# A two-block transformer layer pair on one core: the head of the first block's mixers and of the second block's heads in another order

## The reference, cut to what matters

```python
# block 1: projection of the normed rows; iw are 8 columns per token, g_lr 16
h = rmsnorm(x, norm1_g)
qa, ka, va, iq, ik, iw, qb, kb, vb, g_lr, r_gate = split(h @ w_in)
idx_logits = einsum('bqhd,bsd->bqhs', iq, ik) * IDX_DIM ** -0.5
score = einsum('bqhs,bqh->bqs', relu(idx_logits), iw * IDX_HEADS ** -0.5)
_, idx = top_k(where(causal, score, -inf), 128)           # the keys that attention may see
log_a = log_sigmoid(g_lr @ gla_gate_w2 + gla_gate_b) / 16 # gates of the linear attention
...
# block 2
h = rms_norm(x, g_mix_norm) * (1 + scale_m) + shift_m
q_lat, kv_lat, k_rope, fq, fk, fv, f_logit, gate_a, gate_b = split(h @ w_in_2)
q = rms_norm(q_lat, g_q_lat) @ w_q_up ;  kv = rms_norm(kv_lat, g_kv_lat) @ w_kv_up
q_pe, k_pe = apply_rope(q[..., 64:], positions), apply_rope(k_rope, positions)
cum_log_f = cumsum(log_sigmoid(f_logit + b_forget), axis=1)
```

## Time and profile before

| | before |
|---|---|
| median of 3 runs | 2066.33 us (2064.2 to 2068.21) |
| the profiled execution | 2064.85 us |
| its span in the profile | 2063.0 us, so 1.85 us lie around it |
| PE, DVE, ACT, POOL busy | 92%, 59%, 46%, 30% |
| mean granted clock of TensorE | 0.957 of full |

### The profile page before, as it was taken

How to read it: one execution, slowest core, us unless ns; L and a number is a source line. 1 busy time by engine, 2 the same in 40 slices (tenths; PEclk the granted TensorE clock), 3 DMA queues, 4 the chain that set the end, 5 groups by cost and what they waited for, 6 DMA issues and landing times. The chain is left out here.

```text
span 2063.0 us, 27185 instructions
## 1 busy us (share of the span) xinstructions
PE 1893.1 (92%) x8330; PEld 1306.0 (63%) x8330; DVE 1208.6 (59%) x2231; ACT 953.0 (46%) x1630; POOL 609.2 (30%) x467
## 2 busy tenths in 40 slices
PE   6999998989999995899999969899999999999992
PEld 3534447867777663677678857477766676666661
DVE  1666317367777764563353334477777777776773
ACT  2411227336666553463453222266655565555551
POOL 4797715012222222770100000012222222222221
PEclk9699999989999997999989989999999999999996
DMA  5353410639999964412112354379999999999983
GB/s 183 123 173 104 162 44 12 264 125 332 332 332 333 328 223 149 163 42 91 38 42 86 119 190 177 112 262 343 338 335 324 328 342 332 331 321 330 321 275 103
DMA packets 121435, 441.70 MB, mean 214 GB/s; under 512 B 32036, under 2 KB 36532, under 8 KB 83976
## 3 DMA queue, kind: packets, MB, share of 16 engines
q1 hardware_dynamic: 93672, 406.94, 53.4%
q0 software_dynamic: 27648, 33.67, 7.3%
q10 hardware_dynamic: 32, 0.04, 0.0%
HBM read 446.73 MB, written 63.50 MB: 247 GB/s over the span
## 5 line engine op out<-in xcount | busy, mean ns | idle before, releaser
L1617 DVE TENSOR_TENSOR big_parts<-big,h_cols_parts 128x1024 fp32r<-128x1024 f32 x384 | 460.2, 1222 | 97.1 <-ACT h_cols_parts L1670 87.8
L1670 ACT ACTIVATE h_cols_parts<-big 128x1024 fp32r<-128x1024 f32 x384 | 395.7, 1059 | 65.5 <-PE bank L1576 52.0
L1607 PE MATMUL bank<-big,heads 128*128 128x512 f32 x768 | 352.7, 602 | 1.5 <-ACT heads L1678 1.5
L1884 POOL DMA_INDIRECT acc_scratch<-heads,small x96 | 159.5, 1662 | 615.3 <-DVE small L1648 380.5
L1574 PE MATMUL bank<-h_cols_parts,heads_parts 128*128 128x512 f32 x768 | 309.8, 403 | 4.5 <-DVE heads_parts L1637 4.5
L1576 PE MATMUL bank<-h_cols_parts,heads_parts 128*128 128x512 f32 x768 | 301.5, 393 | 0.0
L1575 PE MATMUL bank<-big_parts,heads_parts 128*128 128x512 f32 x768 | 300.3, 391 | 0.0
L1607 PEld LDWEIGHTS bank<-big,heads 128*128 128x128 f32 x768 | 138.3, 190 | 139.8 <-issue 137.8
L1703 ACT ACTIVATE heads<-bank 128x512 f32<-128x512 f32 x96 | 57.4, 598 | 329.6 <-DMA acc_scratch<-heads,small 251.8
L1574 PEld LDWEIGHTS bank<-h_cols_parts,heads_parts 128*128 128x128 f32 x768 | 145.9, 190 | 31.9 <-DVE heads_parts L1637 5.0
L1576 PEld LDWEIGHTS bank<-h_cols_parts,heads_parts 128*128 128x128 f32 x768 | 144.9, 189 | 31.8
(11 more groups left out here) (410 smaller groups left out, 3059.7 us busy)
## 6 DMA issues: line engine op xcount, KB each, us to landing
big<-in_w_exp_down_dram SPq DMA_DIRECT2D x96, 1024.0 KB
big<-in_w_exp_gate_dram SPq DMA_DIRECT2D x96, 1024.0 KB
big<-in_w_exp_up_dram SPq DMA_DIRECT2D x96, 1024.0 KB
big<-in_w_in_dram SPq DMA_DIRECT2D x13, 2048.0 KB, 8.4
junk<-in_w_mod_dram SPq DMA_DIRECT2D x12, 1024.0 KB, 5.1
spare<-in_w_mod_dram SPq DMA_DIRECT2D x12, 1024.0 KB, 6.9
big<-in_w_out_dram SPq DMA_DIRECT2D x4, 2048.0 KB, 9.4
h_scratch<-h_rows SPq DMA_DIRECT2D x8, 512.0 KB, 2.8
```

The lines of the kernel that those rows point to most:

```text
L1607: mm = pe.matmul(b_y[half][:, :], hidt[:, b, P * j:P * j + P], dn[q][:, j, 512 * half:512 * half + 512], start=j == 0, stop=j == FH - 1)
L1617: dve.tensor_tensor(gu_low[q][:, :, part, :], gu[q][:, :, part, :], gu_high[:, :, part, :].bitcast(F32), ALU.subtract).then_inc(w_low, 1)
L1670: act.activation(gu_high[:, :, part, :], gu[q][:, :, part, :], ACT.Copy).then_inc(w_high, 1)
L1884: return pool.indirect_dma_start(out=K.acc_dram, out_offset=bass.IndirectOffsetOnAxis(at, 0), in_=rows, in_offset=None, bounds_check=S - 1 ...
```

## The change

In `mixers` the low rank product gets eight more weight columns: the indexer's `iw` and `g_lr` lie side by side in the slot, so one unit `low_rank` makes 24 rows. `w2` gets eight rows of zeros in front (a memset of VectorE), so that the gates take all 24 rows. The weights by token are then turned on PE: four transposes into one bank, and one copy with a stride instead of four units of eight products. The order of units becomes `iq0`, `ik`, `low_rank`, `iq1`, and job 0 ends there.

In `first_experts` SyncE issues the five small vectors of block 2 early, then waits for the last scatter to land and issues job 9 alone; job 10 is issued in `later_heads`, after the row tiles, where the vectors were.

In `later_heads` ScalarE's `sines` move up from behind `latent(3)` to before `latent(0)`, and VectorE's `angles` to before `norm(2)`. VectorE rotates one tile ahead of the columns that it copies, and the last step of the logarithms stands after the second rotation. PE makes the forget sums before `turn_heads(3)` (in bank 6 instead of bank 0).

```diff
@@ mixers
-    glr = K.small[0:16, 1024:1536]
+    low_rank = K.small[0:24, 1024:1536]
-    w2 = K.gain[0:16, 768:1024]
+    w2 = K.gain[0:24, 768:1024]
@@ mixers, tensor
             columns("iq0", w, 0, 128, iqT[:, 0, :], scale=32 ** -0.5)
+            pe.wait_ge(key_copies, 2)
+            unit("ik", [(key4[:, c, :], K.ht[:, c, :]) for c in range(KC)], lambda b: b[:, :], ikT)
+
+            columns("low_rank", w, 288, 24, low_rank)
             columns("iq1", w, 128, 128, iqT[:, 1, :], scale=32 ** -0.5)
-            pe.wait_ge(key_copies, 1)
-            unit("ik", [(key4[:, c, :], K.ht[:, c, :]) for c in range(KC)], lambda b: b[:, :], ikT)
-            columns("glr", w, 296, 16, glr)
+            end_job(K)
+            pe.wait_ge(*taken_by("low_rank"))
+            out = claim(len(copies) % 8)
             for t in range(T):
-                unit(f"iw{t}", [(K.ht[:, c, P * t:P * t + P], w[:, c, 288:296]) for c in range(KC)], lambda b: b[:, 0:8],
-                     iw[:, t, :], scale=8 ** -0.5)
-            end_job(K)
+                mm = pe.transpose(out[:, 24 * t:24 * t + 24], low_rank[:, P * t:P * t + P], K.ident[0:24, 0:24])
+            finish(mm, "iw", iw, out[:, 0:96].rearrange("p (t n) -> p t n", t=T)[:, :, 0:8], ACT.Copy, 8 ** -0.5, 0.0, None)
             pe.wait_ge(gate_w_in, 32)
-            pe.wait_ge(*taken_by("glr"))
             for j in range(2):
-                unit(f"gate{j}", [(w2[:, P * j:P * j + P], glr)], lambda b: b[:, :], z[:, j, :], func=ACT.Identity,
+                unit(f"gate{j}", [(w2[:, P * j:P * j + P], low_rank)], lambda b: b[:, :], z[:, j, :], func=ACT.Identity,
                      bias=gate_b[:, j:j + 1])
@@ mixers, vector and sync
+            dve.memset(w2[0:8, :], 0.0).then_inc(key_copies, 1)
-            sp.dma_start(w2, I["gla_gate_w2"][0]).then_inc(gate_w_in, 16)
+            sp.dma_start(w2[8:24, :], I["gla_gate_w2"][0]).then_inc(gate_w_in, 16)
@@ experts_stage, sync
-            if next_jobs:
-                sp.wait_ge(au_mm, E)
-                load_jobs(K, sp, next_jobs)
+            if next_vectors:
+                vectors_in, n = next_vectors(sp)
+                sp.wait_ge(scattered, 16 * E)
+                load_jobs(K, sp, 1)
+                sp.wait_ge(vectors_in, n)
@@ latent_vectors (new): the five loads that stood in later_heads
+    def load(sp):
+        sp.dma_start(K.gq, bcast(I["g_q_lat_2"][0], P)).then_inc(arrived, 16)
+        sp.dma_start(K.gkv, bcast(I["g_kv_lat_2"][0], P)).then_inc(arrived, 16)
+        sp.dma_start(K.b_forget, bcast(I["b_forget_2"][0], P)).then_inc(arrived, 16)
+        sp.dma_start(K.freq, bcast(I["inv_freq"], P)).then_inc(arrived, 16)
+        sp.dma_start(K.pos_i, I["positions_2"][0].rearrange("(t p) -> p t", p=P),
+                     allow_slow_non_contiguous=True).then_inc(arrived, 16)
+        return arrived, 16 * 5
@@ later_heads, tensor
+            def forget_sums():
+                pe.wait_ge(lat_normed, 2 * T + 1)
+                pe.wait_ge(rows_taken, 6 * T - 5)
+                for t in range(T):
+                    for before in range(t + 1):
+                        mm = pe.matmul(K.bank[6][:, 8 * t:8 * t + 8], (K.tri_incl if before == t else K.ones)[:, :],
+                                       fl[:, before, :], start=before == 0, stop=before == t)
+                at_sum.append(product(K, mm))
             turn_heads(2)
+            forget_sums()
             turn_heads(3)
-            pe.wait_ge(rotated, T + 1)
...
@@ later_heads, scalar
             high(1)
+            sines()
             latent(0)
             latent(3)
-            sines()
@@ later_heads, vector
-                if t == 0:
-                    dve.wait_ge(vec_in, 16 * 5)
             low(0)
+            angles()
             norm(2)
             norm_latent(1)
-            angles()
             turn_positions(0)
+            turn_positions(1)
+            dve.wait_ge(lat_std, T + 1)
+            dve.scalar_tensor_tensor(out=fl, in0=fl, scalar=0.0, in1=ftmp, op0=ALU.min, op1=ALU.subtract).then_inc(lat_normed, 1)
             head_columns(0)
-            turn_positions(1)
+            turn_positions(2)
             head_columns(1)
-            turn_positions(2)
+            turn_positions(3)
             head_columns(2)
-            turn_positions(3)
-            dve.wait_ge(lat_std, T + 1)
-            dve.scalar_tensor_tensor(out=fl, in0=fl, scalar=0.0, in1=ftmp, op0=ALU.min, op1=ALU.subtract).then_inc(rotated, 1)
+            dve.wait_ge(K.products, at_sum[0])
+            step(dve.tensor_copy(K.forget, K.bank[6][:, 0:32].rearrange("p (t h) -> p t h", t=T)))
             head_columns(3)
-            dve.wait_ge(K.products, at_sum[0])
-            step(dve.tensor_copy(K.forget, K.bank[0][:, 0:32].rearrange("p (t h) -> p t h", t=T)))
@@ later_heads, sync
-            sp.dma_start(gq, bcast(I["g_q_lat_2"][0], P)).then_inc(vec_in, 16)
...
+            load_jobs(K, sp, 1)
             K.rows2.load(sp, 2)
```

More of the change, by code:

```diff
@@ L1504, in hier_router, with experts_stage @@
     return load, vectors, scalar, vector
-def experts_stage(K, tag, m, weights, init, next_jobs=0):
+def experts_stage(K, tag, m, weights, init, next_vectors=None):
     nc, E = K.nc, m.E
@@ L1885, in scatter_add, with latent_vectors @@
                                    bounds_check=S - 1, oob_is_err=False, compute_op=ALU.add)
+def latent_vectors(K):
+    I, small = K.I, K.small
+    arrived = K.sem("lat_vectors_arrived")
+    K.gq, K.gkv, K.b_forget = small[:, 0:256], small[:, 256:384], small[:, 384:392]
+    K.pos_i, K.freq = small[:, 512:516].bitcast(I32), small[:, 520:536]
+    def load(sp):
[6 more added lines that the diff above has]
+        return arrived, 16 * 5
+    return load
 def first_experts(K):
     m, I = K.m1, K.I
-    experts_stage(K, "moe1", m, K.moe1, [(K.rows_stored, 16 * T), (K.acc_set, 16 * T)], next_jobs=2)
+    experts_stage(K, "moe1", m, K.moe1, [(K.rows_stored, 16 * T), (K.acc_set, 16 * T)],
+                  next_vectors=latent_vectors(K))
     overflow_stage(K, "moe1", m, I["w_exp_gate"], I["w_exp_up"], I["w_exp_down"])
@@ L1991, in later_heads @@
     h_high_ready, h_low_ready = s("h2_high"), s("h2_low")
-    vec_in, sin_in, sin_out = s("lat_vectors_arrived"), s("lat_angles_ready"), s("lat_sines_ready")
+    sin_in, sin_out = s("lat_angles_ready"), s("lat_sines_ready")
     lat_taken, lat_squares, lat_std = s("lat_taken"), s("lat_squares"), s("lat_std_and_log")
-    lat_normed, turned = s("lat_normed"), s("lat_turned_copied")
-    rows_taken, rotated = s("up_taken"), s("up_rotated_and_logf")
+    lat_normed, turned = s("lat_normed_and_logf"), s("lat_turned_copied")
+    rows_taken, rotated = s("up_taken"), s("up_rotated")
     columns = (s("mla_columns_act"), s("mla_columns_dve"))
@@ L2004, in later_heads @@
     square_out = scr[:, 4240:8336].rearrange("p (t d) -> p t d", t=T)
-    gq, gkv, b_forget = small[:, 0:256], small[:, 256:384], small[:, 384:392]
+    gq, gkv, b_forget = K.gq, K.gkv, K.b_forget
     lat_ss, lat_sd, lat_rs = (small[:, a:a + 8].rearrange("p (t n) -> p t n", t=T) for a in (392, 400, 408))
@@ L2008, in later_heads @@
     K.forget = small[:, 480:512].rearrange("p (t h) -> p t h", t=T)
-    pos_i, pos = small[:, 512:516].bitcast(I32), small[:, 516:520]
-    freq = small[:, 520:536]
+    pos_i, pos, freq = K.pos_i, small[:, 516:520], K.freq
     ss, sd, rs = (small[:, a:a + 4] for a in (536, 540, 544))
@@ L2119, in _ @@
             turn_heads(2)
+            forget_sums()
             turn_heads(3)
-            pe.wait_ge(rotated, T + 1)
-            for t in range(T):
-                for before in range(t + 1):
-                    mm = pe.matmul(K.bank[0][:, 8 * t:8 * t + 8], (K.tri_incl if before == t else K.ones)[:, :],
-                                   fl[:, before, :], start=before == 0, stop=before == t)
-            at_sum.append(product(K, mm))
         def copy_columns(eng, copy, which, t):
@@ L2321, in _ @@
                 sp.dma_start(K.hr[:, t, :], K.acc_dram[P * t:P * t + P, :]).then_inc(x_in[t], 16)
-            sp.dma_start(gq, bcast(I["g_q_lat_2"][0], P)).then_inc(vec_in, 16)
-            sp.dma_start(gkv, bcast(I["g_kv_lat_2"][0], P)).then_inc(vec_in, 16)
-            sp.dma_start(b_forget, bcast(I["b_forget_2"][0], P)).then_inc(vec_in, 16)
-            sp.dma_start(freq, bcast(I["inv_freq"], P)).then_inc(vec_in, 16)
-            sp.dma_start(pos_i, I["positions_2"][0].rearrange("(t p) -> p t", p=P),
-                         allow_slow_non_contiguous=True).then_inc(vec_in, 16)
+            load_jobs(K, sp, 1)
             K.rows2.load(sp, 2)
```

## The result

The changed kernel takes 2046.91 us (median of 4 runs, 2042.01 to 2049.55) where the kernel before, beside it, took 2065.26 (4 runs). The ratio is 0.9900 (95%: 0.9883 to 0.9917); a second set of runs gave 0.9895 (0.9878 to 0.9911).

What follows compares the result with a forecast made beforehand. In the mixers PE and GpSimd run as two tied chains; around 800 us no engine is full and PE waits for VectorE's rotations. -7.5 - 4.8 = -12.3 from 2064.85 gives 2052.5, median 2054.0 us; range 2047 to 2060.5.

Steps and rivals of the forecast that it cites:

- Part A: Start of the mixers: iw units go, four turns come, VectorE scores earlier; -7.5 us (-5 to -9.9).
- the 13 units: Mixers: the score units VectorE must do before PE finishes its scores; 8.0 us of work, 14.7 us of time.
- rival 4: Mixers: PE waits longer for GpSimd and the clock's fall outlasts the following units; at 30 us of loss 2069; chance 0.04.
- The full lock (rival 1): Mixers: each score waits out a whole GpSimd instruction; the mixers give only 2.5 us, time 2059; chance 0.10.
- Rival 3: Mixers: without the 8-column units the clock stays at 2.4 GHz through scoring; time 2049.5; chance 0.14.
- part B: From the last scatter to the first attention of block 2: 0.7 + 0.9 - 1.15 - 5.2 = -4.8 us.
- Rivals 2 and 5: 2: loads and heads give nothing, 2058.8, chance 0.10. 5: new waits before gate0 and in the barrier, 2064, chance 0.04.
- The start, +0.7: Last scatters to first split: barrier ends 1.1 us earlier, but ScalarE waits for job 9; +0.7 us (-1.1 to +2.5).
- The front, +0.9 and -1.15: Start of the heads: table change for the early sines costs +0.9 us; VectorE's wait for the sines returns 1.15.
- The end, -5.2: End of the heads: forget sums lie in PE's wait, rotations come earlier, last column copy added; -5.2 us (-3 to -7.5).

Runs made afterwards that it cites:

- mixers alone: The kernel before with only the mixers' edits (low rank product with indexer weights, four turns, moved ik, iq1, end of job): 0.9977 of the kernel before, median 2061.31 us.
- run with filler: The changed kernel without rotation ahead, plus three 512-column matmuls on PE between forget sums and last turns: fox begins 75.6 us after the first turn, 77.8 without them.

## Why the prediction was right or wrong

**Part A, -7.5: right in mechanism; that the size is near is in part luck.** By the earlier trace rows: First score forecast at 56.5, found at 55.5 (54.7 to 56.2 in all profiles with the change): the gates ran at full clock. `mod_sum` 0 comes 10.6 us earlier (four profiles against eight with part A as it is), where I had 7.8. Of the difference 1.0 is the first score and 1.9 the 13 units behind it, which took 12.8 us instead of 14.7: I used the speed of 256 columns for the 384 ones too. (My own 71.2 + 2.6 is 73.8 and not the 73.5 that I went on with, so the sum was really 7.5 there.) As forecast, GpSimd then decides: its pause is gone, and PE's earliness above GpSimd's is lost at `mod_sum` 3. The loss has a second half that I priced at nothing. The wait is longer there (4.6 to 5.4 us against 2.5 to 3.2), and `mod_sum` 3 now mostly runs at half clock (1.87 + 1.86 us against 1.02 + 1.01), as rival 4 had it in small. So -10.6 + 2.1 + 1.7 = -6.8 at the loop, two misses that nearly cancel. This is the mean over the profiles (148.4 against 155.2 us); the pair that I had to compare shows -8.6, since the profile of before that I read has the latest loop of its four.

**The full lock (rival 1)** is out: scores were at 1.06 and 1.03 us, and one-input multiplies hardly block. **Rival 3** is out in its condition: the clock fell in scoring all the same (`mod_sum` 0 at 1.87 us), and at the same time as before, just before 56 us, although no 8-column units stand there now. It only came back earlier. By stretches of 2 us the granted clock is 0.50 from 56 to 78 us and 1.00 from 80 us on; in the kernel before it is 0.50 up to 88 us and 1.00 from 90. Over the stretch of the earlier trace rows:

```profile
55.00:87.00 32.00, 32.00 (x63) 13.19 (x62) 28.46 (x41) 18.27 (x32) 30.18 (x21) 0.63 0.43 152
```

(That is the row of all engines from 55 to 87 us; the granted clock is the third number from its end.) The time came out near its 2049.5, but from part B, not from this. Rivals 2 and 5, which end above 2058, are out, and of rival 4 only the small loss at `mod_sum` 3 came.

**Part B, -4.8: wrong in size; about -11.** By its terms:

- *The start, +0.7: the step that failed in sign.* I added job 9's two issues and ScalarE's wait for its landing, and took the gain of the freed queues only in the scatters. Measured: -2.3. Two terms were off. The last two steps of the scatters got 4.7 us shorter (16.2 to 11.5 on average) and not 2.4, as they are 5.4 to 6.3 us apart, not 6.5. And ScalarE's wait for job 9, 1.8 us in the sum, didn't come: the second transfer landed 8.9 us after the first issue (I had 9.1), but the barrier let ScalarE begin 9.5 us after it and not 7.3, so the data was there 0.6 us before. What holding job 9 back costs at the barrier, 1.6 us, is near the 1.27 that I used. (These terms and the -2.3, counted from ScalarE's last copy, start at different points and don't add exactly.) My sign for this step, the split 9 to 10 us after the last landing, came true with 9.5 us, by luck: the wait that it stood for isn't in it.
- *The front, +0.9 and -1.15: right together.* From first square to first turn it is 46.0 to 46.4 us (47.4 and 47.5 in two profiles), and was 45.8 and 46.8 in the two profiles with the old order and loads: no difference that these tell, where I had -0.25. Inside, both terms are larger: the table loads came as named (805.16 and 811.71), and the turning of the third tile's latents is 2.1 us later after the first square, not 0.9; but PE's wait before the first turn is 1.51 us instead of 3.08.
- *The end, -5.2: mis-sized.* It is 19.3 us instead of 26.9 and 26.0: -6.7 to -7.6. The steps were right (sums under the rotation's wait, hardly a wait left before the turns), but I counted the turn of 3.44 us as if it would stay. Behind waits of 3 us the first turns ran at half clock (3.45 us before, 3.65 in mixers alone), and so did the last in the kernel before (3.44), though not in mixers alone (1.95); in the changed kernel each takes 1.9, which is 1.5 us less. GpSimd's last half, which I named as the cover that might be missing, ended at 857.34 in the changed kernel, 2.15 us before the attention begins, with SyncE's issue for its next half among the last things of the stage: not the bound, but near it.
- *Missing altogether, -1.7:* "nothing behind 875 us changes but its start". The attention's four warm-up products start at the clock that the stage before leaves: 3.65 us against 1.96. The run with filler shows that this and the turns are the clock, not the work. In the kernel before, the slow warm-up goes with the sums' place, as the run that has them last shows.

**The sum** by these, with -7.2 for the end: -6.8 - 2.3 - 7.2 - 1.7 = -18.0, against -17.2 in the profiled pair. The terms at the end and behind it hold most of the miss: 3.7 of the 6.4 us by which part B was too small; the start has 3.0, and the front takes 0.3 back. What I chose badly was to forecast the clock only as a rival in the mixers and never as a term in the heads, though the rows of half clock stood in the group I quoted.

## What to carry to other kernels

Where a wait of PE of some us is removed, look at the durations behind it too: if the same operation stands in the profile with two durations, the longer one is part of the wait's price, and it can reach into the next stage. When two chains are tied at several points, relaxing one moves the bound to the next tie; here a sum asked for 7 us later brought as much as the whole new order of the indexer. And a load issued in a stage's tail costs what it holds up there, and holding it back costs what its issue then adds before the barrier: here the two were equal for job 9, and only the load whose data is needed last was worth moving.

## What the runs showed of the hardware

In the heads, a wait of PE of 2.3 to 3.1 us was followed by turns wholly or partly at half clock in six cases (2.81 to 3.65 us), by turns of 2.11 us in one and of 1.95 us in two; waits up to 1.9 us left them at 1.91 to 2.11, except where the forget sums, products of 8 columns, stood just before (0.98 us of wait, then 3.65).

A VectorE operation with one SBUF tensor as input also waits for GpSimd's adds: 384 columns took 0.41 us beside an idle GpSimd and 1.42 beside adds. It is one that takes 0.35, 0.41 and 0.48 us for 256, 384 and 512 columns, so about half as much for each further column as the two-input one (0.57, 0.71 and 0.87 us).

The stage of the 64 experts, which moves its weights at 318 to 344 GB/s in most of its stretches, took 731 to 737 us in profiles of kernels that don't differ in it (from its first instruction to the end of the span). From the loop over chunks to the first square, where only the order of loads in the tail differs, it was 641 to 649. So a few us of any total are chance; stage starts compare better than totals.
